# Prompt attention: one order of the steps for all engines, or one for each engine

## The reference

```python
p_c = masked_softmax(einsum('bqhgd,bchd->bqhgc', qs, kv_cmp[:, :, 0]), m_c)     # compressed keys, 16 blocks
o_c = einsum('bqhgc,bchd->bqhgd', p_c, kv_cmp[:, :, 1])
p_s = masked_softmax(einsum('bqhgd,bqhkd->bqhgk', qs, kv_sel[..., 0, :]), m_s)  # selected keys: all earlier ones
o_s = einsum('bqhgk,bqhkd->bqhgd', p_s, kv_sel[..., 1, :])
p_w = masked_softmax(einsum('bqhgd,bkhd->bqhgk', qs, kv_band[:, :, 0]), m_w)    # window of 512 keys
o_w = einsum('bqhgk,bkhd->bqhgd', p_w, kv_band[:, :, 1])
return gates[..., 0:1] * o_c + gates[..., 1:2] * o_s + gates[..., 2:3] * o_w
```

## Time and profile before

| | |
|---|---|
| median of 3 runs | 1014.05 us (1013.36 to 1018.79) |
| profiled execution, its own time | 1020.7 us |
| its span, first to last instruction | 1019.0 us |
| mean granted TensorE clock | 0.958 of full |
| TensorE busy | 935.7 us (92%) |
| VectorE, ScalarE, GpSimd busy | 595.0, 409.7, 190.9 us |
| attention of the prompt | 283 to 721 us |

### The profile page before, as it was taken

The page is one execution under the profiler, slowest core; times in us unless marked ns, Lnnn a source line. Parts: engine busy times, 40 slices in busy tenths (PEclk is TensorE's granted clock), DMA queues, the critical chain, the costliest instruction groups (busy, mean ns, idle before and its releaser), DMA issues. The chain is left out here.

```text
span 1019.0 us, 16705 instructions
## 1 busy us (share of the span) xinstructions
PE 935.7 (92%) x5935; PEld 808.9 (79%) x5935; DVE 595.0 (58%) x1428; ACT 409.7 (40%) x916; POOL 190.9 (19%) x178
## 2 busy tenths in 40 slices
PE   5999999998989988999999988999688999999997
PEld 5999999998979887777889867777445666777665
DVE  6531010194444576878555668787567867787653
ACT  6432111111023454666534445667264434434322
POOL 0049599999010000000000230000000000000000
PEclk9999999998999999999999979999688999999999
DMA  7127534534052101000011013300533455452321
GB/s 252 53 97 241 194 114 147 175 118 125 1 169 67 48 16 36 1 1 1 9 43 50 23 39 101 108 1 1 191 91 103 128 166 163 139 160 68 116 89 32
DMA packets 106820, 93.73 MB, mean 92 GB/s; under 512 B 21245, under 2 KB 99954, under 8 KB 104626
## 3 DMA queue, kind: packets, MB, share of 16 engines
q1 hardware_dynamic: 84946, 58.65, 19.1%
q10 hardware_dynamic: 19488, 17.25, 5.6%
q0 software_dynamic: 2304, 16.78, 4.8%
HBM read 78.16 MB, written 18.61 MB: 95 GB/s over the span
## 5 line engine op out<-in xcount | busy, mean ns | idle before, releaser
L592 PE MATMUL ps<-w_hi,h_hi 128*128 128x264 f32 (+5 forms) x432 | 123.9, 287 | 0.2 <-DVE h_lo L464 0.2
L592 PE MATMUL ps<-w_lo,h_hi 128*128 128x264 f32 (+5 forms) x432 | 122.9, 284 | 0.0
L592 PE MATMUL ps<-w_hi,h_lo 128*128 128x264 f32 (+5 forms) x432 | 122.8, 284 | 0.0
L1269 DVE TENSOR_TENSOR pt_lo<-ps,pt_hi 128x512 fp32r<-128x512 f32 x132 | 90.9, 689 | 52.0 <-ACT pt_hi L1190 51.4
L1190 ACT ACTIVATE pt_hi<-ps 128x512 fp32r<-128x512 f32 x132 | 78.6, 597 | 83.2 <-PE ps L1099 82.3
L472 DVE TENSOR_TENSOR w_lo<-w_raw,w_hi 128x1024 fp32r<-128x1024 f32 (+3 forms) x13 | 33.6, 2585 | 128.0 <-ACT w_hi L366 128.0
L1265 DVE TENSOR_REDUCE least<-ps 128x1 f32<-128x640 f32 (+7 forms) x128 | 90.0, 703 | 14.1 <-PE ps L1088 12.9
L313 POOL TENSOR_TENSOR chunk<-chunk 128x1024 f32<-128x1024 f32 (+2 forms) x46 | 82.5, 1793 | 3.6
L592 PEld LDWEIGHTS ps<-w_hi,h_hi 128*128 128x128 f32 (+1 forms) x432 | 79.6, 184 | 0.5 <-issue 0.4
L592 PEld LDWEIGHTS ps<-w_lo,h_hi 128*128 128x128 f32 (+1 forms) x432 | 79.6, 184 | 0.0
L592 PEld LDWEIGHTS ps<-w_hi,h_lo 128*128 128x128 f32 (+1 forms) x432 | 79.3, 184 | 0.0
(11 more groups left out here) (379 smaller groups left out, 2257.4 us busy)
## 6 DMA issues: line engine op xcount, KB each, us to landing
kv_pages<-in_cache_slc_kv SPq DMA_DIRECT2D x256, 64.0 KB, 1.9
shared<-in_x_prompt SPq DMA_DIRECT2D x8, 512.0 KB, 3.6
w_raw<-in_w_in SPq DMA_DIRECT2D x8, 512.0 KB, 3.9
wr_raw<-in_w_in SPq DMA_DIRECT2D x8, 512.0 KB, 4.0
kv_window<-in_cache_win_kv SPq DMA_DIRECT2D x4, 1024.0 KB, 5.8
wo_raw<-in_w_out SPq DMA_DIRECT2D x8, 512.0 KB, 9.0
out<-in_cache_win_kv SPq DMA_DIRECT2D x1, 4032.0 KB
x_row<-in_x_prompt ACTq DMA_DIRECT2D x7, 512.0 KB, 4.2
```

The source lines that it names most:

```text
L592: mm = nc.tensor.matmul(out, lhs, rhs, start=(k == 0 and i == 0), stop=(k == KD - 1 and i == 2))
L1269: nc.vector.tensor_tensor(pt_lo[:, t % PTS, :], ps[:, turn_bank(t), :], pt_hi[:, t % PTS, :].bitcast(F32), ALU.subtract).then_inc(s_ptl, 1)
```

## The change

The planner of the last stage is moved out to the top of the file as `arrange` (with `sorted_by_need`). It gets one more argument, `from_pe`, an extra lag where the step waited for is TensorE's, and a need on the same engine has no hand-over any more. The prompt stage gets costs (`parts`) and needs (`needs`) for its steps, groups the same steps into eight lists by kind, and lets the planner order them for each engine. TensorE, ScalarE and VectorE walk their own order; SP still walks `steps`, and `place`, the order of use of the spare bank, is still taken from `steps`. Two waits are added.

```diff
+def arrange(lists, parts, needs, handover, from_pe, window):
+    heads, after, before = {}, {}, {}
+    for n, steps in enumerate(lists):
+        for step in steps:
+            done = None
+            for eng, cost in parts(step):
+                key = step, eng
+                line = heads.setdefault((n, eng), [])
+                before[key] = [((s, e), lag + (0.0 if e == eng else handover + (from_pe if e == "PE" else 0.0)))
+                               for s, e, lag in needs(step, eng)]
+                if done:
+                    before[key].append((done, handover + (from_pe if done[1] == "PE" else 0.0)))
+                if line:
+                    before[key].append((line[-1][0], 0.0))
+                line.append((key, cost))
+                done = key
...
+    def place(first, then, rank, window):
+        missing = {key: len(first.get(key, [])) for key in cost}
+        ready = dict.fromkeys(cost, 0.0)
+        open_to = {eng: [key for key in cost if key[1] == eng and not missing[key]] for eng in ENGINES}
+        free, at = dict.fromkeys(ENGINES, 0.0), {}
+        while len(at) < len(cost):
+            begin = lambda key: max(free[key[1]], ready[key])
+            soonest, eng = min((min(map(begin, keys)), eng) for eng, keys in open_to.items() if keys)
+            key = min((key for key in open_to[eng] if begin(key) <= soonest + window), key=rank)
+            open_to[eng].remove(key)
+            at[key] = free[eng] = begin(key) + cost[key]
...
+    forward = place(before, after, lambda key: -left[key], 0.0)
+    backward = place(after, before, lambda key: -forward[key], 0.0)
+    at = place(before, after, lambda key: -backward[key], window)
+    return {eng: [key[0] for key in sorted((k for k in at if k[1] == eng), key=at.get)] for eng in ENGINES}
...
+    FIRST_REST = sum(1 for s in steps[:at["scores", PER_KV // 2, 0]] if s[0] == "rest") // KD
...
+        if what == "scores":
+            chunks = [min(512, n - c) for c in range(0, n, 512)]
+            edges = 2 if x % 2 == 1 and x % PER_KV // 2 >= WIN // P else 1
+            return (("PE", sum(2 * max(0.112, c * 0.000456) for c in chunks) + 0.09 * edges),)
+        full = {
+            "k_stage": (("DVE", 0.65),) if x == 0 else (),
+            "k_turn": (("PE", 0.45), ("ACT", 0.6), ("DVE", 0.7)),
+            "c_keys": (("PE", 1.8), ("ACT", 0.2), ("DVE", 0.18)),
+            "c_rows": (("PE", 1.8), ("DVE", 0.5)),
+            "v_stage": (("ACT", 0.62), ("DVE", 0.69)),
+            "w_split": (("ACT", 0.41), ("DVE", 0.42)),
+            "rest": (("PE", 0.5),),
+            "rest_out": (("ACT", 0.47), ("DVE", 0.54)) if what == "rest_out" and is_gate(x) else (("ACT", 0.47),),
+            "query": (("PE", 0.45), ("ACT", 0.6), ("DVE", 1.3)),
+            "c_scores": (("PE", 0.9), ("DVE", 0.6)),
+            "c_exp": (("ACT", 0.27), ("DVE", 1.05)),
+            "c_turn": (("PE", 0.11), ("DVE", 0.29)),
+            "c_values": (("PE", 0.3), ("DVE", 0.43)),
+            "least": (("DVE", 0.15 + 0.00105 * n),),
+            "exp": (("ACT", 0.42 + 0.00083 * n),),
+            "turn": (("PE", 0.44), ("ACT", 0.6), ("DVE", 0.69)),
+            "sum": (("PE", 0.47), ("ACT", 0.6)) if what == "sum" and y == tiles_of[x] - 1 else (("PE", 0.47),),
+            "output": (("PE", 0.9), ("DVE", 1.2)),
+        }
...
+        if eng == "PE" and (what, x) in spare_before and spare_before[what, x]:
+            k, n = spare_before[what, x]
+            on(spare_step[k], n, 0, "DVE")
+        if what == "k_turn" and eng == "PE":
+            if y >= 2:
+                on("k_turn", x, y - 2, "DVE")
+            elif x > 0 and y == 0:
+                u = PER_KV * x - 2
+                on("turn", u, tiles_of[u] - 1, "DVE")
+                on("scores", u + 1, NG - 1, "PE")
...
+            if y == 0 and x == FIRST_REST:
+                on("exp", PER_KV - 1, NG - 1, "ACT")
...
+            if tiles_of[x] > 4:
+                last = (FIRST_REST if kv == 0 else ITEMS) - 1
+                taken(last)
+                taken(last - 1)
...
+    order = arrange([of("k_stage", "k_turn", "c_keys", "c_rows"), of("v_stage"), of("scores", "least", "exp"), of("turn"), of("sum"),
+                     of("query", "c_scores", "c_exp", "c_turn", "c_values", "output"), of("rest", "rest_out"),
+                     of("w_split")], parts, needs, 0.15, 0.2, 0.3)
...
-    for what, x, y in steps:
+    for what, x, y in order["PE"]:
...
                         if y == 0:
                             pe.wait_ge(s_exp, NG * (x + 1))
+                            if x % PER_KV == PER_KV - 1 and x + 1 < UNITS:
+                                pe.wait_ge(s_klo, 6 * ((x + 1) // PER_KV) + 6)
...
-                for what, x, y in steps:
+                for what, x, y in order["ACT"]:
...
+                            if is_gate(x - 1):
+                                act.wait_ge(s_rt, x)
...
-                for what, x, y in steps:
+                for what, x, y in order["DVE"]:
...
-    order = schedule()
+    order = arrange([list(decays()), list(linear()), list(sample_states()), [s for pi in range(PAIRS) for s in pair(pi)], list(project_out()), list(gated(LASTM)), list(split_out())], parts, needs, 0.15, 0.0, 0.3)
```

More of the change, by code:

```diff
@@ L82, in wait, with sorted_by_need @@
         self.eng.wait_ge(self.sem, at if self.it is None else self.it * self.per + at)
+ENGINES = "PE", "ACT", "DVE", "SP"
+def sorted_by_need(keys, before):
+    out, seen = [], set()
+    for key in keys:
+        todo = [key]
+        while todo:
+            k = todo[-1]
+            wait = [b for b, _ in before[k] if b not in seen]
+            if wait:
+                todo += wait
+            else:
+                todo.pop()
+                if k not in seen:
+                    seen.add(k)
+                    out.append(k)
+    return out
@@ L760, in attend_prompt @@
     place = {x: n for n, x in enumerate(uses)}
+    FIRST_REST = sum(1 for s in steps[:at["scores", PER_KV // 2, 0]] if s[0] == "rest") // KD
+    spare_before = {}
+    for n, (k, x) in enumerate(uses):
+        what = {"q": "query", "cs": "c_scores", "ct": "c_turn", "co": "c_values", "z": "output"}[k]
+        spare_before[what, x] = uses[n - 1] if n else None
+    spare_step = {"q": "query", "cs": "c_scores", "ct": "c_turn", "co": "c_values", "z": "output"}
+    is_gate = lambda n: REST[n // NCH3][0] == "gate"
@@ new lines, in parts @@
+    def parts(step):
+        what, x, y = step
+        n = tiles_of[x] * P if what in ("scores", "least", "exp") else 0
+        if what == "scores":
[22 more added lines that the diff above has]
+        }
+        return full[what]
@@ L762, in turn_bank @@
+    of = lambda *names: [s for s in steps if s[0] in names]
+    order = arrange([of("k_stage", "k_turn", "c_keys", "c_rows"), of("v_stage"), of("scores", "least", "exp"), of("turn"), of("sum"),
+                     of("query", "c_scores", "c_exp", "c_turn", "c_values", "output"), of("rest", "rest_out"),
+                     of("w_split")], parts, needs, 0.15, 0.2, 0.3)
     def turn_bank(t):
@@ L1781, in needs @@
         return out
[L1783 to L1797, removed]
```

140 lines of the change are left out of this document (93 added, 47 removed).

## The result

The changed kernel takes 958.41 us in the median against 1014.61, a ratio of 0.943 (95% interval 0.940 to 0.947): 56 us less. The forecast was 988 with a range down to 965. The direction was right; of the gain that came, the 26 us forecast were less than half.

A forecast was written before the change was run, and what follows sets the result against it. TensorE was taken to bound the prompt stage, 366 us of work in 438, idling through waits of order, not capacity. Order 20 plus clock 6 gave 26 us: 1014.05 - 26 = 988 us, range 965 to 1019.

The forecast's parts named there:

- The order term: Prompt stage, one order per engine: 20 of TensorE's 24.7 us of spare-bank waits go, none of the other 14.6; bounds 0 and 39.
- The clock term: TensorE in the prompt stage: 6 of the 17 us lost at the lower clock behind stalls come back; bounds 0 and 17.
- The small gaps: TensorE in the prompt stage: 16 of the 72 us beyond its work are gaps too small to be listed, given no gain.
- Rest work: Leftover projection items, second 11: spread beside narrow tiles up to 616 us; part of the 26 us already credited, not more.
- the balance is reached: Rival: planner fills prompt stretches to 95% and 91% of TensorE's work, stage 393 us, time 969 or 965; chance 0.12.
- The waits move: Rival: tile loop sets the pace, spare-bank waits reappear at L1099 and L1110; 1009 to 1017 us, say 1012; chance 0.15.
- too tight: Rival: planned order without slack, VectorE stands before late pt_lo in the 64 wide heads; up to 1032 us; chance 0.15.
- Queues: SP's queue keeps the old list in the prompt stage; stores and weight loads keep their sequence, so nothing is passed.
- added waits: Next head's c_rows before a kv head's last-unit transposes: cost 0, at worst 4 us; ScalarE on s_rt: once, half a microsecond.
- the last stage: Planner call without 0.15 us on same-engine needs: some places may swap, up to 3 us either way, taken as 0.
- The cover: SP's window load for the next stage, issued behind rest: 16 us remain before the prompt stage's end, hiding it.
- POOL beside VectorE: POOL's block slows some dozen small products, 229 ns against 165: under 1 us, taken as 0; by the skill's rule 5 us.

The follow-up runs named there:

- float_rest: Changed kernel with only rest, rest_out and w_split placed freely by the planner; spare-bank chain and all other prompt steps in the old order: 977.98 us, ratio 0.965.
- float_spare: Changed kernel with only the spare-bank chain (query, c_scores, c_exp, c_turn, c_values, output) placed freely, all other prompt steps in the old order: 967.41 us, ratio 0.955.
- float_both: Changed kernel with spare-bank chain, rest groups and weight splits placed freely; heads, turns and sums keep the old interleave in one list: 963.28 us, ratio 0.950.
- long_stalls: Changed kernel with four stops of TensorE, 2.57 us each, in the first wide stretch while GpSimd clears a tile: 970.64 us, ratio 0.956.
- tail_before: Changed kernel with the last stage's order of before (0.15 us again on needs on the same engine in that planner call): 957.19 us, ratio 0.943.
- one_order: Changed kernel with all prompt steps in one planner list, so every engine keeps the old order there; added waits stay: 1014.39 us, ratio 1.000.

## Why the prediction was wrong, point by point

- **The bound.** "TensorE is the fuller engine, its work is 366 us of 438, the waits are of order, not of capacity" was right: the stage now takes 376 us with the same instructions.
- **The order term, the step that failed most.** 20 us of 39.3 us of idle were credited: four fifths of the spare-bank waits and "none of the other 14.6, which are the tile loop's own hand-overs". After, none of the 24.7 is left, and 5.6 of the 14.6. A wait of TensorE is idle only if nothing else is ready. I sorted the idle time by the step that ended it, and treated each name as a separate cause. float_rest shows that the names are not causes: the spare-bank chain keeps its place there, and its waits fall from 24.7 to 9.0 us. float_spare and float_both show the other half: with the tile loop in one list, 12.8 and 10.4 of the 14.6 stay, and they go only when heads, turns and sums are parted as well. The term should have been the idle time less the start and the end of the stage, 34 us.
- **The clock term.** 6 of 17 us were credited, "because other small gaps stay and can fall as badly". All 17 came back in the profile. The small gaps did not stay, and long_stalls shows the link to stops (falls behind three of four stops of 2.57 us). But the link is not one to one: of the falls before, the one at 511 us stands behind c_keys and c_rows, which the changed kernel runs too, without a fall, while float_spare and long_stalls have one there. So some of the 17 in this one execution, 3.5 us below its median, is likely luck. The argument from 402 to 498 us, which lost 2%, was a misreading: that stretch was not full, it had TensorE idle for 6.7 us.
- **The small gaps.** The 16 us called "gaps too small to be listed" got no credit. In the profiles 376.4 - 366 - 5.6 = 5 us of such are left, so 11 went. The two levels are rough, since the costs overstate the work (the first stretch takes 100 us where they sum to 105); the 11 don't depend on that.
- **Together** 34 + 17 + 11 + 3 of the last stage are the profiles' 65, of which 56 remain in the medians. The difference of 10 lies in the profiled executions (6 us above the median before, 3.5 below after). The last stage's 3 are part of it: tail_before and one_order show no gain there.
- **Rest work.** "Part of the 26 already credited, not more" failed: floated alone it gives 36 us.
- **The rival "the balance is reached"**, 965 to 969 us at a chance of 0.12, was nearest. Its fills of 95% and 91%, work over length, were too low for the stage as a whole, which reached 366 / 376 = 97%: 82 of 85 us in the first wide stretch, though only 82 of 96 in the second. "Two engines at 90% with two score buffers rarely fit" was wrong: VectorE is at 91% of the first one (77.19 of 85) beside a full TensorE. "The waits move" and "too tight" did not come about: pt_lo's wait for pt_hi fell from 51.4 to 17.1 us, and between the stage's start and its end TensorE never waits more than 0.5 us.
- **Queues, added waits, the last stage** as predicted: nothing passed, one_order at 1.000 with the added waits, tail_before at no difference.
- **The cover** held, 32.6 us where 16 were forecast, but not by its reasoning: rest was to end 30 us later and ended 21 us sooner, and the stage ended 62.4 us sooner instead of 26. That the two errors left the sum positive is luck.
- **POOL beside VectorE** cost less than the hint: 166 ns. I also took the preparation of the next keys between units 14 and 15 for a move; the old order already had it there, at 497.72 us, and only the wait for it is new.

What stays open: why the planned order fails as one list as badly as 1009.6 or 1020.2 us. Two ways of cutting it were tried, a better cut of all eight lists was not. Open too is what decides whether a stop is followed by a fall of the clock.

## What to carry to other kernels

When an in-order engine has enough work for the whole stage, and its stalls end at many different steps, don't price a new order by the stalls that it names: bound it by the sum of the engine's work, plus start and end, at the full clock (366 + 5.6 here, against 376.4 reached). Let one kind of independent work float first; that may already bring most of it (here 36 and 47 of 56 us), and the gains of several kinds don't add. Give each engine its own order and plan them together: one engine's alone brought 13 or 18 us, and one common list at best 26.

## What the runs showed of the hardware

The clock of TensorE kept its full level over 376 us in an execution in which the engine, after its start, had no idle gap longer than 0.8 us. A stop of 0.8 us brought no fall in four cases, one of 2.57 us a fall in three of four, one of 1.75 us in two of three in the kernel before. Falls also came with no idle time before them, behind 32 matmuls of 2 and 64 columns (long_stalls at 294 us, float_spare at 486); the changed kernel ran the same step with none. Each of these single falls cost 1.7 us ((1 - 0.57) x 4).
